# Value products of the first mixer in unsplit fp32 on 64 rows, and more of its convolution's taps on VectorE

## The reference, cut to what matters

```
px, ph = xm @ w_in, hm @ w_in                # 512 q, 128 k, 128 v, 1024 for the GLU
qx, kx = apply_rope(...), apply_rope(...)    # latent tokens; 8 query heads, 2 key heads of 64
ax = window_gqa(qx, kx, vx, kh, vh, sink, scale)   # latent: |i-j| <= 128 plus all context; sink logit
ah = attend(qh, kh, vh, None, sink, scale)         # context: context alone
y = a * sigmoid(g)                                 # 512 channels, 512 tokens
y = depthwise convolution of 31 taps + b_dw        # latent and context apart
bx = silu(layer_norm(y, ln_g, ln_b))
ox = concatenate([ax, bx]) @ w_out                 # the same for ph
```

## Time and profile before

| | us |
|---|---|
| median of 3 runs | 1679.69 (1679.23 to 1680.28) |
| profiled execution | 1684.07 |
| its span, first to last instruction | 1682.2 |
| TensorE busy | 1649.3 |
| VectorE busy | 1132.4 |
| ScalarE busy | 603.7 |
| GpSimd busy | 126.2 |
| first mixer, value transposes to output products | 424 to 573.4 |

### The profile page before, as it was taken

One profiled execution on the slowest core, in us unless ns is written; L12 is line 12 of the kernel. 1 busy time (PEld: TensorE's weight loads), 2 busy tenths in 40 slices (PEclk: granted clock), 3 DMA queues, 4 the chain that ended last, 5 costly groups with the idle time before them and its releaser, 6 DMA issues.

```text
span 1682.2 us, 23652 instructions
## 1 busy us (share of the span) xinstructions
PE 1649.3 (98%) x8871; PEld 1414.0 (84%) x8871; DVE 1132.4 (67%) x1885; ACT 603.7 (36%) x817; POOL 126.2 (8%) x81
## 2 busy tenths in 40 slices
PE   8999999999999899999999999999999999999998
PEld 6788888889877698888888898888888888989997
DVE  5878777777585678787787873463333687666665
ACT  3321222223776532212212342212222356444443
POOL 0000000000796100000000000000000011000000
PEclk7999999999999999999999999999999999999999
DMA  7754554542211035555555323342222231155552
GB/s 296 281 202 181 194 198 187 204 150 97 101 51 50 26 133 189 191 189 210 190 197 191 139 75 121 149 149 84 104 88 100 101 105 72 50 183 197 184 198 75
DMA packets 45426, 247.45 MB, mean 147 GB/s; under 512 B 5168, under 2 KB 5296, under 8 KB 25008
## 3 DMA queue, kind: packets, MB, share of 16 engines
q1 hardware_dynamic: 45360, 246.55, 40.2%
HBM read 245.48 MB, written 1.05 MB: 147 GB/s over the span
## 4 chain that ended last, share of the span: by engine, by line
PE 89%; DVE 5%; POOL 2%; issue 2%; ACT 1%; DMA 0%; SPq 0%; ACTq 0%; POOLq 0%; DVEq 0%
PE ps L1828 13%; PE ps L1830 13%; PE ps L1837 13%; PE ps L1659 10%; PE ps L1661 10%; PE ps L1660 10%; PE ps L2303 5%; PE ps L1686 4%; PE ps L2309 2%; POOL spare L571 2%; PE ps L1945 1%; PE ps L1866 1%; PE ps L2026 1%; DVE w_lo L1221 1%; PE ps L1900 1%
## 5 line engine op out<-in xcount | busy, mean ns | idle before, releaser
L1828 PE MATMUL ps<-a_hi,w_hi 128*128 128x512 f32 x960 | 373.8, 389 | 0.8 <-ACT w_hi L687 0.8
L1830 PE MATMUL ps<-a_lo,w_hi 128*128 128x512 f32 x960 | 373.5, 389 | 0.0
L1221 DVE TENSOR_TENSOR w_lo<-raw,w_hi 128x2048 fp32r<-128x2048 f32 x114 | 260.5, 2288 | 49.3 <-ACT w_hi L687 21.7
L1659 PE MATMUL ps<-h_hi,w_lo 128*128 128x512 f32 (+1 forms) x648 | 234.9, 362 | 1.5 <-POOL h_lo L577 1.4
L1661 PE MATMUL ps<-h_hi,w_hi 128*128 128x512 f32 (+1 forms) x648 | 233.4, 360 | 0.0
L1660 PE MATMUL ps<-h_lo,w_hi 128*128 128x512 f32 (+1 forms) x648 | 233.4, 360 | 0.0
L1837 PE MATMUL ps<-a_hi,w_lo 128*128 128x512 f32 x960 | 227.3, 389 | 0.0
L1828 PEld LDWEIGHTS ps<-a_hi,w_hi 128*128 128x128 f32 x960 | 180.2, 188 | 38.9 <-issue 0.8
L1837 PEld LDWEIGHTS ps<-a_hi,w_lo 128*128 128x128 f32 x960 | 180.2, 188 | 37.4
L1830 PEld LDWEIGHTS ps<-a_lo,w_hi 128*128 128x128 f32 x960 | 180.2, 188 | 37.3
L681 ACT ACTIVATE work<-ps 128x512 f32<-128x512 f32 x66 | 39.5, 599 | 431.2 <-PE ps L1837 418.7
(11 more groups left out here) (344 smaller groups left out, 2525.7 us busy)
## 6 DMA issues: line engine op xcount, KB each, us to landing
raw<-wstream SPq DMA_DIRECT2D x147, 1024.0 KB, 4.9
mring<-wmod SPq DMA_DIRECT2D x144, 512.0 KB, 3.5
spare<-wstream SPq DMA_DIRECT2D x11, 1024.0 KB, 4.8
xT<-tokens SPq DMA_DIRECT2D x4, 512.0 KB, 5.1
cb<-cond SPq DMA_DIRECT2D x1, 1024.0 KB, 8.0
out<-mring SPq DMA_DIRECT2D x4, 256.0 KB, 2.1
mring<-gain SPq DMA_DIRECT2D x1, 512.0 KB, 6.5
cst<-consts SPq DMA_DIRECT2D x1, 449.0 KB, 7.0
```

The costliest lines, as they stand in the source:

```text
L1221: dve.tensor_tensor(w_lo[:, slot], raw[:, slot], w_hi[:, slot].bitcast(F32), ALU.subtract).then_inc(lo_ready, 1)
L1659: pe.matmul(dst, lhs_lo, rhs_hi, start=start, stop=False, skip_group_check=True)
L1828: pe.matmul(bank, hi, a_hi[:, k, 0:nt], start=k == 0, stop=False, skip_group_check=True)
L1830: pe.matmul(bank, hi, a_lo[:, k, 0:nt], start=False, stop=False, skip_group_check=True)
```

## The change

It does four things, all in the first mixer. (1) The values are turned from an fp32 copy `ab_v` and not split, the turned probabilities (`ab_pt`) are copied once by ScalarE and not split, and a pair's value products are unsplit fp32 products with 64 rows of output each, one unit of the pair above the other (`unit_outputs`); both units' outputs then lie in one range of columns and VectorE scales them with one instruction. (2) The spread (`unit_spreads`) goes to its own columns and is issued behind the value products of the pair ahead, one pair earlier than it is used; ScalarE copies it behind the exponential and the probabilities' copy of its loop, and waits for the outputs of the pair ahead. (3) TensorE does 16 taps of tile 2; slab `CB` is gone and the others move up; ScalarE adds the bias in place in bank 5 at i = 14, and VectorE adds taps 16 to 30 of tile 2 there. (4) VectorE has 20 instead of 15 taps of tile 3, so GpSimd makes 40 adds. The orders `TAPS_AT`, `ADDS_AT`, `POOL_SLABS` follow; the second slab of outputs is copied at i = 18 in one piece.

```diff
-W_FFN1 = W_AB + 9 + 4
+W_FFN1 = W_AB + 8 + 4
...
-            ab_pt_hi = sb("ab_pt_hi", [P, 2, 2, TOK], F32R, where=turned)
-            ab_pt_lo = sb("ab_pt_lo", [P, 2, 2, TOK], F32R, where=turned)
+            ab_pt = sb("ab_pt", [P, 2, 2, TOK], where=turned)
+            ab_v = sb("ab_v", [P, TOK], where=turned)
...
-        OWN_TAPS = 15
+        OWN_TAPS, PE_TAPS = 20, 16
         CONV_ADDS = 2 * (TAPS - 1) - OWN_TAPS
-        DVE_TAPS = TAPS + OWN_TAPS + 1
+        REST_FROM = TAPS + OWN_TAPS
+        REST_TO = REST_FROM + TAPS - PE_TAPS
+        DVE_TAPS = REST_TO + 1
...
-        TAPS_AT = (1, 3, 4, 4, 4, 4, 4, 4, 3, 2, 3, 1, 3, 3, 2, 1, 0, 0, 0, 1)
+        TAPS_AT = (1, 3, 4, 4, 3, 4, 4, 4, 4, 4, 4, 2, 4, 4, 3, 3, 2, 3, 3, 3, 1)
         ADDS_FIRST = 6
-        ADDS_AT = (2, 1, 3, 3, 1, 2, 3, 3, 1, 2, 3, 3, 2, 3, 0, 3, 0, 3, 1)
+        ADDS_AT = (2, 1, 3, 3, 1, 2, 3, 3, 1, 3, 3, 2, 2, 2, 2, 1)
...
-        POOL_SLABS = {1: G3, 4: CA, 8: Q23, 14: CB, 16: W_AB + 9, 23: W_AB + 10}
+        POOL_SLABS = {1: G3, 4: CA, 8: Q23, 15: W_AB + 8, 19: W_AB + 9}
...
             for i in range(len(units) + 6):
-                if i >= 5 and i % 2 and (i - 5) // 2 < AB_PAIRS:
-                    p = (i - 5) // 2
-                    n = P * len(units[2 * p][1])
-                    r0 = spread_at(p)
-                    act.wait_ge(spread_done, p + 1)
-                    if p >= 2:
-                        act.wait_ge(o_scaled, p - 1)
-                    act.activation(rspread[:, p % 2, 0:n], ps[AB_O_BANK][:, r0:r0 + n], ACT.Copy).then_inc(spread_copy, 1)
...
-                    act.activation(pt_unit(AB_PT[0], e, units[e][1]), pt_bank(e, units[e][1]),
+                    act.activation(pt_unit(AB_PT, e, units[e][1]), pt_bank(e, units[e][1]),
                                    ACT.Copy).then_inc(pt_hi, 1)
+                if i >= 5 and i % 2 and (i - 5) // 2 < AB_PAIRS:
+                    p = (i - 5) // 2
+                    n = P * len(units[2 * p][1])
+                    act.wait_ge(spread_done, p + 1)
+                    if p >= 1:
+                        act.wait_ge(o_scaled, p)
+                    act.activation(rspread[:, p % 2, 0:n], ps[AB_O_BANK][:, LAT:LAT + n], ACT.Copy).then_inc(spread_copy, 1)
...
+                    act.activation(ps[5][:], ps[5][:], ACT.Identity, bias=vec[:, V_BDW + 2:V_BDW + 3],
+                                   scale=0.5).then_inc(conv_copy, 1)
...
-                if 3 <= i < len(units) + 3:
-                    e = i - 3
-                    qts = units[e][1]
-                    dve.wait_ge(pt_hi, e + 1)
-                    dve.tensor_tensor(pt_unit(AB_PT[1], e, qts), pt_bank(e, qts),
-                                      pt_unit(AB_PT[0], e, qts).bitcast(F32), ALU.subtract).then_inc(pt_lo, 1)
...
+                    dve.wait_ge(spread_copy, p + 1)
                     dve.wait_ge(pv_done, p + 1)
-                    dve.wait_ge(spread_copy, p + 1)
+                    dve.wait_ge(spread_done, min(p + 2, AB_PAIRS))
...
-                        last = dve.tensor_tensor(onorm[rows, p % 2, 0:n], ps[AB_O_BANK][rows, u * n:(u + 1) * n],
-                                                 rspread[rows, p % 2, 0:n], ALU.mult)
-                    last.then_inc(o_scaled, 1)
+                    dve.tensor_tensor(onorm[:, p % 2, 0:n], ps[AB_O_BANK][:, 0:n], rspread[:, p % 2, 0:n],
+                                      ALU.mult).then_inc(o_scaled, 1)
...
+            def unit_outputs(p):
+
+                qts = units[2 * p][1]
+                n = len(qts) * P
+                turned_pair = AB_PT[p % 2].rearrange("p a n -> p (a n)")
+                tiles = TOK // n
+                for k in range(tiles):
+                    for u in range(2):
+                        v, c = qts[0][1] + k * P + A_DIM * u, (2 * k + u) * n
+                        last = pe.matmul(ps[AB_O_BANK][A_DIM * u:A_DIM * (u + 1), 0:n], ab_v[:, v:v + A_DIM],
+                                         turned_pair[:, c:c + n], start=k == 0, stop=k == tiles - 1,
+                                         skip_group_check=True)
+                last.then_inc(pv_done, 1)
...
                 if i >= 5 and i % 2:
-                    p = (i - 5) // 2
...
-                    pe.wait_ge(pt_lo, 2 * p + 2)
-                    pe.wait_ge(spread_copy, p + 1)
...
+                    pe.wait_ge(pt_hi, i - 3)
+                    pe.wait_ge(spread_copy, (i - 5) // 2 + 1)
+                    unit_outputs((i - 5) // 2)
+                if i >= 3 and i % 2 and (i - 3) // 2 < AB_PAIRS:
+                    pe.wait_ge(rinv_ready, (i - 3) // 2 + 1)
+                    unit_spreads((i - 3) // 2)
```

More of the change, by code:

```diff
@@ L202, in build @@
         kr_even, kr_odd = q_lo[:, 6], q_hi[:, 6]
-        AB_PT = [(x[:, 0], x[:, 1]) for x in (ab_pt_hi, ab_pt_lo)]
+        AB_PT = (ab_pt[:, 0], ab_pt[:, 1])
         O_TILE = (6, 7, 0, 1)
@@ L288, in build @@
         v_copy = sem("v_copy")
+        v_turned = sem("v_turned")
         ot_hi = sem("ot_hi")
@@ L1304, in dve_taps @@
                 for n in range(first, last):
[L1305 to L1306 removed]
                     if n:
                         dve.wait_ge(conv_op, n)
[L1309 removed]
+                    if n == REST_TO:
                         dve.wait_ge(tap_add, CONV_ADDS)
[L1311 removed]
+                        dve.tensor_tensor(conv[:, 3], ps[LN_BANK][:], conv[:, 3], ALU.add).then_inc(conv_op, 1)
                         continue
+                    c, tap = dve_tap(n)
+                    sums, whole = tap_view(ps[5 if c == 2 else LN_BANK][:]), tap_view(conv[:, c])
+                    if n == REST_FROM:
+                        dve.wait_ge(conv_copy, 1)
                     x, col = ypad[:, c, :, tap:tap + LAT], vec[:, V_WDW + c * TAPS + tap:V_WDW + c * TAPS + tap + 1]
@@ L2014, in query_products, with conv_products @@
                         ins.then_inc(slab_done if t else step_done, 1)
-            def conv_products(slab, tap0, tap1, first, last):
-                order = [(part, tap) for part in (0, 1, 2) for tap in range(tap0, tap1)]
+            def conv_products(first, last):
+                order = [(part, tap) for part in (0, 1, 2) for tap in range(PE_TAPS)]
                 for part, tap in order[first:last]:
-                    if (part, tap) == (0, tap0):
-                        pe.wait_ge(hi_ready, slab + 1)
-                    if (part, tap) == (2, tap0):
-                        pe.wait_ge(lo_ready, slab + 1)
+                    if (part, tap) == (0, 0):
+                        pe.wait_ge(hi_ready, CA + 1)
+                    if (part, tap) == (2, 0):
+                        pe.wait_ge(lo_ready, CA + 1)
                     lhs, rhs = (w_lo if part == 2 else w_hi), (y_lo if part == 1 else y_hi)
-                    c0 = (tap - tap0) * P
-                    ins = pe.matmul(ps[5][:].rearrange("p (v n) -> p v n", v=2), lhs[:, slab % 2, c0:c0 + P],
+                    c0 = tap * P
+                    ins = pe.matmul(ps[5][:].rearrange("p (v n) -> p v n", v=2), lhs[:, CA % 2, c0:c0 + P],
                                     rhs[:, :, tap:tap + LAT], start=part == 0 and tap == 0,
-                                    stop=part == 2 and tap == TAPS - 1, skip_group_check=True)
-                    if (part, tap) == (2, tap1 - 1):
+                                    stop=part == 2 and tap == PE_TAPS - 1, skip_group_check=True)
+                    if (part, tap) == (2, PE_TAPS - 1):
                         ins.then_inc(slab_done, 1)
@@ L2078, in early_out, with unit_spreads @@
                            h_hi[:, O_TILE[k]], h_lo[:, O_TILE[k]], k == 0, False)
+            units = AB_UNITS
+            def unit_outputs(p):
[10 more added lines that the diff above has]
+                last.then_inc(pv_done, 1)
+            def unit_spreads(p):
+                for b in range(len(units[2 * p][1])):
+                    c = LAT + b * P
+                    for u in range(2):
+                        col = units[2 * p + u][2][b]
+                        last = pe.matmul(ps[AB_O_BANK][A_DIM * u:A_DIM * (u + 1), c:c + P],
+                                         rinv[:, col:col + 1].to_broadcast([P, A_DIM]), ident,
+                                         start=True, stop=True, skip_group_check=True)
+                last.then_inc(spread_done, 1)
             EARLY = {21: (0, (0, 1)), 23: (1, (0,)), 25: (1, (1,)), 27: (2, (0, 1))}
-            units = AB_UNITS
             for i in range(len(units) + 4):
@@ L2118, in _ @@
                     last.then_inc(pt_done, 1)
-                if i >= 5 and i % 2:
-                    p = (i - 5) // 2
-                    pe.wait_ge(rinv_ready, p + 1)
-                    if p >= 1:
-                        pe.wait_ge(o_scaled, p)
-                    for b in range(len(units[2 * p][1])):
-                        c0 = spread_at(p) + b * P
-                        for u in range(2):
-                            col = units[2 * p + u][2][b]
```

(4 more changed lines are left out.)

130 lines of the change are left out of this document (44 added, 86 removed).

## The result

The changed kernel takes 1684.34 us, median of 16 runs (1682.09 to 1686.26), the kernel before 1680.0, timed beside it: ratio 1.002, 95% interval 1.0014 to 1.0027. It is slower: by 2.4 to 4.5 us by the interval, 4.3 by the medians. I had forecast 1678.5. Its profiled execution took 1685.06 us, 0.7 above its median, where that of the kernel before lay 4.4 above its own.

The account below looks back on a forecast made before the run. TensorE was taken as busy for 98% of the span, with GpSimd also full up to unit 11. Terms: 0 - 1.0 - 2.7 + 1.5 + 0 + 1 = -1.2; 1684.07 - 1.2 - 4.4 = 1678.5 us, range 1670 to 1687.

Parts of the forecast that it names:

- To unit 12: Stretch up to unit 12's first score product: GpSimd's adds still end near 499.9 us; total 0, bounds -0.5 and +2.
- Rival D: Before unit 12, pairs wait for the late copy of the spread: +1 for each of three, 1682 us; chance 0.06.
- Units 12 to 15: Stretch of 21.05 us: TensorE gains 2 x 0.55, ScalarE runs later; -1.0, bounds -2.5 and +0.5.
- Units 16 to 19: Stretch of 22.8 us: 10.4 us of products removed buy -2.7 at the upper clock; a low clock adds +1.5.
- The chain: Dependent steps in units 16 to 19: 11.7 us against 13.75 for units 16 and 17, otherwise 8.3 against 9.03.
- Units 20 to 27: Stretch of 26.9 us: 26.8 expected, total 0 at the upper clock, +1 partly at the lower; bounds -4 and +6.
- the clock's terms: Additions for TensorE's lower clock: +1.5 in units 16 to 19 (one or two pairs), +1 in units 20 to 27.
- rival B: Lower clock from unit 16 to the mixer's end and into the output products: +7, about 1685.5 us; chance 0.18.
- The last line: Forecast time: profiled execution 1684.07, minus 1.2 for the change, minus 4.4 from profile to runs' median: 1678.5 us.
- The copy of the spread: ScalarE's copy, moved behind the exponential: some 1.5 us later in odd units; mean product 8.8 us behind unit 20's scores.
- Rival A: TensorE's saving kept from unit 12 on: units 16 to 19 18 us, last stretch 24; -8, 1671.7 us; chance 0.30.
- Rival C: Value products' 64-row halves don't overlap: 0.85 us more per pair, on the chain in 8; +7, 1685.5 us; chance 0.04.

Follow-up runs that it names:

- products_in_the_waits: The changed kernel with 28, 12, 9 and 9 unread products ahead of the value products of units 17, 19, 21 and 23: 1679.11 us.
- before_products_ahead: The kernel before with 6 unread products behind unit 11 and 9 in unit 17 ahead of its spread: 1679.39 us.
- before_again: The kernel before, unchanged, in a second profiled execution: 1681.82 us in place of 1684.07.
- first_and_products: rspread_first with 22, 6, 2 and 6 unread products ahead of the value products of units 17, 19, 21 and 23: 1672.6 us.
- rspread_first: The changed kernel with ScalarE's copy of the spread put back to the head of its loop iteration, before the exponential: 1672.66 us.
- before_products_in_waits: The kernel before with 6 unread products behind unit 11 and 9 in unit 17 behind its spread: 1682.54 us.
- halves_in_a_row: rspread_first with the two halves of the value products one after the other instead of in turn: 1675.24 us.

## Why the prediction missed

Times of the profiled executions, in us; the forecast's own steps, at the upper clock and with its clock terms:

| | before | forecast | the change | the change without drops | before without drops |
|---|---|---|---|---|---|
| unit 12's scores | 502.7 | 502.7 | 501.8 | 502.3 | 503.4 |
| units 12 to 15 | 21.05 | 20.05 | 19.25 | 19.3 | 19.5 |
| units 16 to 19 | 22.8 | 20.1 + 1.5 | 22.9 | 19.9 | 21.2 |
| units 20 to 27 | 26.9 | 26.8 + 1 | 30.5 | 27.3 | 26.9 |
| outputs start | 573.4 | 572.2 | 574.45 | 568.8 | 571.0 |

(The last two columns are products_in_the_waits and before_products_ahead; "without drops" holds from unit 12 to the output products.)

**To unit 12, forecast 0:** -0.9, outside the bound of -0.5; but before_again has unit 12's scores at 502.1, so 0.6 of it is what executions of one kernel differ by. TensorE waited 2.2 us for the copy at unit 5, and a drop stands behind that wait near 472 us (clock 0.97 in the first window). Neither made unit 12 later: GpSimd is busy for 53.5 of the 58 us here too. Rival D did not come.

**Units 12 to 15, forecast -1.0:** -1.8, inside the bounds, but in part by luck: before_again, without the drop behind unit 12, takes 19.4 us and the change 19.25. Nearly all of the 1.8 is that drop, and the two shorter value blocks, counted at 1.1, show 0.15.

**Units 16 to 19, forecast -2.7 and +1.5.** The chain was right: unit 16's scores to unit 18's took 11.6 us at the upper clock (forecast 11.7), the next pair 8.3 (8.3). The clock was not: the stretch cost 3.0 us more with its two drops, twice the +1.5. The price of a drop was right: the forecast's 1.06 for the value block and 0.4 for the scores make 1.5 for one pair and 2.9 for two. I wrote "one or two pairs" and summed one.

**Units 20 to 27, forecast 0 and +1.** Again the chain held: mean product 8.6 us behind unit 20's scores where I said 8.8, the whole 27.3 against 26.8. With the drops 30.5: the clock's term was 3.2, not 1.

**The step that failed** is thus the clock's terms in both stretches, +1.5 and +1: I counted too few drops, about one for each stretch where there were two. The terms measured 3.0 and 3.2 us, and with unit 16's scores 0.5 apart the output products start 5.6 us later (574.45 - 568.8); the medians differ by 5.2. I had written rival B for this: +7, 1685.5 us, if the clock is low for over 20 us. It was low for 20.5 of 53, and the time is 1684.3. That B came so near is in part luck. B had one lower stretch to the mixer's end and into the output products; there were four, the last over at 566 us. It set the clock 7 us above the forecast; the runs showed 3.7 (6.2 - 2.5), and another 3.7 came from the offset below. What misled me was my sentence against it, that before TensorE was busy 78% of the last 26.4 us without a drop. That is an average. The change kept the share near that (71% of 30.5 us) but gathered the idle time in single waits before the value products, of 3.6 to 8.3 us, where before had 3.0 at most, and a drop begins in each of these waits or right behind it. The runs give no length of wait that decides it: behind 2.2 us at unit 25 first_and_products has one and rspread_first none. That the lower clock for 20 us or more would make the prediction wrong stood in its last lines.

**The last line, 1684.07 - 1.2 - 4.4,** failed with it. I took the offset between profile and median over unchanged. It was mostly the lower clock too: before's two waits of 1.9 and 3.0 us bring a drop in some executions, and with both filled (before_products_ahead) no run lies above 1680.83 us. The profiled execution of before also has a drop near 1480 us, far behind the mixer, and takes 1.6 us longer there than before_products_ahead's. The changed kernel's waits brought their drops in both executions profiled, so its profile lies only 0.7 above its median. Of the 5.8 us between forecast and measurement 2.2 are the sum against profiled executions, and the larger part, 3.7, is this offset; which drops each timed run had, no profile shows.

**The copy of the spread.** I had priced its delay inside the chains, and rightly, as their lengths show. But I set it against the gains and left it, where it was the largest term of the change: 11.7 us. Rival A (-8, 1671.7 us: 18 us for units 16 to 19 and 24 for the last stretch) comes near what rspread_first gives: 17.5, 22.7 and 1672.7. That the times agree is in part luck, since A's also holds the offset of 4.4. Nothing in VectorE's order had to change for it, only one place in ScalarE's, so the order that the argument against A speaks of was the one of the wrong engine. How the 11.7 us divide between waits and clock can be estimated only: at the upper clock units 16 to 19 take 19.9 with the late copy and 16.4 with the early one, the last stretch 27.3 and 22.7, so 8.1 together are waits.

**Rival C:** a value block takes 0.89 us to its spread (519.85 to 520.74); refuted. The rule that I cited for C (the Trainium skill, TensorE: Matmul & The Clock Gate, Part 3, The mechanism: a weight load runs under matmuls only if its row group differs) does not describe these rows. All products of the block use all 128 rows of the array, and the 16 weight loads of unit 19's block in rspread_first lie within 0.88 us, under its products.

## What to carry to other kernels

Before pricing what a change removes, list every operation that it moves in an engine's order, and ask which wait now stands ahead of it: here the place of a copy of 0.3 us, behind a wait for another engine, outweighed 10.4 us of products. Look at TensorE's idle time wait by wait, the longest first, and not only by its share of a window; where a forecast says "one or two" drops, work out both sums. Do not carry an offset between one profiled execution and the median over to the changed kernel if its waits differ: here 4.4 us became 0.7.

## What the runs showed of the hardware

Products that nobody reads, put into TensorE's waits, made the changed kernel 5.2 us faster by keeping the granted clock at 2.4 GHz; put behind a wait nine of them cost their full length, 2.1 us (before_products_in_waits), and with the copy early they gained nothing that can be told (1672.6 and 1672.66 us).

Products that write different column halves of the array do not keep the program's order between the halves: in halves_in_a_row three records of the spread (537.55, 537.71 and 537.82) start ahead of the last value product's records, which stand before them in the program (to 537.87). The Trainium skill (TensorE: Matmul & The Clock Gate, Part 3, The mechanism) says that matmuls start and end strictly in program order; the starts in this trace differ, and of the ends it can say nothing sure, since they are modelled.
